# Whole-unit quanta for the last third of a dense projection that is woven into attention and a gated recurrence

## The chip, the cores and the metric

The kernel runs on one core of a Trainium2 chip (trn2). The metric is the device time of one execution in microseconds (us), as the median of three runs. The profiled execution is one of its own; its time and its span are given apart.

## The reference, cut to what matters

One inference step of a hybrid encoder layer on 2048 prompt frames and 32 new frames of a running stream (2080 rows of width 1024). After an RMSNorm one input projection feeds three head groups; their outputs are joined, projected and passed through a squared-ReLU MLP.

```
p = einsum('btd,de->bte', xn, w_in)          # 7 column groups of 512
qa, ka, va | qb, kb, vb | qc, fc, ic, gc = split(p)
oa = stick_breaking_attention(qa, ka, va)
ob = chunk_band_attention(qb, kb, vb, bias)
# HGRN2, per head a 128 x 128 state S, blocks of frames in order:
A   = (q_i * k_j * decay_ij) summed over k;  o = A v + (q exp(G)) S
S   = exp(G_last) * S + (k exp(G_last - G))^T v
oc  = rmsnorm(o) * onorm * silu(gc)
h   = x + concat(oa, ob, oc) @ w_o;  y = h + relu(rmsnorm(h) @ w_up)^2 @ w_down
```

All matrix products of the projections run as three products of a high and a low part (xhi.whi, xlo.whi, xhi.wlo), since the result has to hold float32 accuracy.

## The kernel before, in words

Three stages follow each other. `front` normalises x, keeps its transposed high and low parts and makes three of the seven column groups (QKA, VQ, KV) of the projection. `middle` is the stage of the change. `merge_and_ffn` is w_o and the MLP.

In `middle` four streams of work share all engines. **B** and **A** are the two attentions, one after the other; **C** is the recurrence (HGRN2) over 17 tiles (16 of 128 frames, one of 32), which starts when A is done. **D** (`dense`) makes the other four groups QC, FC, IC, GC that C reads, in three thirds of the rows (tiles 0 to 5, 6 to 11, and 12 to 16 with 544 columns). D's results go to memory (`scratch_tr`, `scratch_proj`) and C loads them from there tile by tile.

A D **unit** is one output block: 24 matmuls that add up in one PSUM buffer psD (8 parts of the depth times 3 products). For IC and GC a unit is 128 (or 32) rows by 256 columns, for QC and FC 128 by 272 columns in the last third. Units of one third, group and half of the columns form a **piece** (4 or 5 units in the last third), which shares one 1 MB weight load and its split into high and low parts. A unit is cut into **quanta**, stretches of matmuls that are issued together. Before, each unit of the last third has 3 quanta of 8 matmuls.

The order is written out by hand. Each stream is a generator per engine that yields after each turn. `interleave` in `middle` lays a turn of A, B or C and so many turns of D behind it into one list, `plan`, and all five engines walk through this same list. A turn of D is one quantum. What the other engines do for a unit is counted from its last quantum `z`: at turn z+1 (EVAC) ScalarE moves psD into one of three output buffers `ob` (for GC a sigmoid into `sg`); at z+2 (REFINE) VectorE works on FC or multiplies psD by the sigmoid for GC (signal `gated`); at z+3 (ONORM) GpSimd multiplies GC by a gain; at z+4 (STORE) SyncE issues the store. ScalarE waits before EVAC of unit n for the store of unit n-3. TensorE has two psD buffers, so before unit n it waits for EVAC of unit n-2, or for `gated` of unit n-2 if that is a GC unit (L645 on). SyncE loads a piece's weights at the first quantum of the piece ahead of it, first thing in the turn, after waiting for the last unit of the piece before that; the split of the weights comes at quanta 6 to 9 of that piece (`split_at`).

The last A turns belong to no new attention unit; they drain what is under way: the last transpose back (L1196), the copy L1102, the store L897. A has 196 turns and 10 quanta of the last third lie beside its last 9. C then takes a **spot** per turn, 9 spots per tile. C's first 88 spots carry the rest of D; the spots after that have none. At a spot there is a product on TensorE (L1514, 4 matmuls, one per head); one spot on, VectorE and GpSimd merge its factors into the operands of the same tile's next product (L1431, L1433, L1363), which comes two spots after, and VectorE puts the result in place (L1445, "take"). Tiles overlap, so that 8 of 9 spots have a product. Further come a transpose (L1524), the product with v (L1549, L1552), the state (L1533, L1461) and the norm and gate (L1409, L1471, L1479, L1379). SyncE loads a tile's five arrays (L1323 to L1326) 13 spots ahead.

Of the kernel before, what the change touches and what calls it, by code (L numbers as in the profile page):

```python
# [409 lines left out]
def dense(nc, sems, mp, xhi, xlo, xt, w_in, lower_bounds, onorm, psD, proj, tr):  # L410
# [31 lines left out]
    pieces, units, quanta = [], [], []  # L442
    for t, tiles in enumerate(THIRDS):
        base, n = tiles[0][0], sum(r for _, r in tiles)
        for g in ORDER[t]:
            for c in range(2):
                first = len(units)
                if g in (QC, FC):
                    for e in range(2):
                        for c0, cn in blocks_of(n):  # L450
                            units.append((t, g, 2 * c + e, base + c0, cn, len(pieces), 4 if cn > 300 else 3))
                else:
                    for t0, r in tiles:
                        units.append((t, g, c, t0, r, len(pieces), 3))
                pieces.append((t, g, c, first, len(units) - 1))
    begins, ends = [], []
    for n, u in enumerate(units):
# [6 lines left out]
    TURNS = NQ + STORE + 1  # L464
    piece_begin = [begins[p[3]] for p in pieces]

    SPLIT = 6
    split_at = {}
    for q in range(1, len(pieces)):
        for j in range(4):  # L470
            split_at[piece_begin[q - 1] + SPLIT + j] = (q, j)

    def tile_index(t, t0):
        return [z[0] for z in THIRDS[t]].index(t0)
# [22 lines left out]
    def stored_count(n):  # L497
        return 16 * sum(n_stores(k) for k in range(n % NO, n + 1, NO))
# [69 lines left out]
    def scalar(act):  # L568
        def split(q, j):
            if j == 0:  # L570
                act.wait_ge(w_loaded[q % 2], 16 * (q // 2 + 1))
                if q >= 2:
                    act.wait_ge(unit_done, pieces[q - 2][4] + 1)
            nc.scalar.activation(whi[q % 2][:, 2 * j:2 * j + 2, :], wst[q % 2][:, 2 * j:2 * j + 2, :], ACT.Copy
                                 ).then_inc(whi_ready, 1)

        for j in range(4):
            split(0, j)
        act.wait_ge(lchain, 1)
        nc.scalar.activation(lexp[:, :], lsm[:, :], ACT.Exp).then_inc(lexp_ready, 1)  # L580
        for z in range(TURNS):
            n = unit_end.get(z - EVAC)
            if n is not None:
                t, g, c, t0, r, _, _ = units[n]
                b = n % NO
                act.wait_ge(unit_done, n + 1)
                if n >= NO:

                    act.wait_ge(stored[b], stored_count(n - NO))
                ps = psD[n % NB]  # L590
                if g == QC:
                    last = nc.scalar.activation(ob[b][:, 0:r], ps[:, 0:r], ACT.Copy, scale=float(P) ** -0.5)
                elif g == FC:
                    nc.scalar.activation(ob[b][:, 0:r], ps[:, 0:r], ACT.Sigmoid)
                    last = nc.scalar.activation(sg[b][:, 0:r], ps[:, 0:r], ACT.Sigmoid, scale=-1.0)
                elif g == IC:
                    last = nc.scalar.activation(ob[b][0:r, 0:256], ps[0:r, 0:256], ACT.Copy)
                else:
                    last = nc.scalar.activation(sg[b][0:r, 0:256], ps[0:r, 0:256], ACT.Sigmoid)
                last.then_inc(act_evac, 1)  # L600
            if z in split_at:
                split(*split_at[z])
            yield

    def vector(dve):
# [20 lines left out]
        for z in range(TURNS):  # L626
            n = unit_end.get(z - REFINE)
            if n is not None:
                t, g, c, t0, r, _, _ = units[n]
# [7 lines left out]
                elif g == GC:  # L637
                    dve.wait_ge(act_evac, n + 1)
                    nc.vector.tensor_tensor(ob[b][0:r, 0:256], psD[n % NB][0:r, 0:256], sg[b][0:r, 0:256], ALU.mult
                                            ).then_inc(gated, 1)  # L640
            if z - 1 in split_at:
                split(*split_at[z - 1])
            yield

    def tensor(pe):  # L645
# [1517 lines left out]
```

## Time and profile before

| | |
|---|---|
| median of 3 runs | 3165.74 us (3161.7 to 3167.32) |
| profiled execution, its own time | 3159.14 us |
| its span on the core | 3157.4 us |
| mean granted TensorE clock | 0.977 of full |
| TensorE busy | 2965.0 us (94%) |
| VectorE busy | 1647.3 us (52%) |
| ScalarE busy | 957.8 us (30%) |
| GpSimd busy | 327.8 us (10%) |
| `middle`, A's last turns | about 1066 to 1080 us of the span |
| C with D beside it | 1087.4 to about 1275 us |
| C alone | about 1275 to 1396 us |

The busy shares say where to look at all: TensorE is busy nearly everywhere, and the stretches in which it isn't are few. They do not say what the change is worth, since the change moves matmuls from one stretch to another and removes none. That is read from the stretches themselves.

### The profile page before, as it was taken

Reading aid. Unit: us, or ns where it says so; the run is one execution under the profiler, and the core shown is the slowest. Engines: PE = TensorE matmul, PEld = TensorE weight load, DVE = VectorE, ACT = ScalarE, POOL = GpSimd, SP = SyncE. Lnnn points to the kernel's source line nnn. Section 1 sums busy time; section 2 is a strip of 40 time slices with the busy share of each in tenths; the row PEclk is TensorE's granted clock in tenths of the full one; section 3 lists DMA queues with packets and bytes.
Section 4 is the critical chain, followed back from the end, with each engine's and each line's share of the span. In section 5 each row is a group of like instructions: output and inputs, shape, how many; then the busy total and the mean of one; then the engine's idle time right before and its main releaser. Section 6 shows DMA issues by size and latency. Waiting matters only on the chain.

```text
span 3157.4 us, 45442 instructions
## 1 busy us (share of the span) xinstructions
PE 2965.0 (94%) x18200; PEld 2620.7 (83%) x18200; DVE 1647.3 (52%) x2241; ACT 957.8 (30%) x1621; POOL 327.8 (10%) x504
## 2 busy tenths in 40 slices
PE   6999799899999999859999999989999999899999
PEld 4678578788888899757889999879998998788887
DVE  4545244366566578863445444534544545455554
ACT  3322155445555322122312222222221222322221
POOL 1222110021000145630000000000000000000000
PEclk9999899999999999979999999999999999999999
DMA  6652322246222544322212112222121213222221
GB/s 207 195 188 101 101 81 75 84 131 169 79 78 72 173 144 127 116 107 87 94 54 77 57 54 94 103 71 94 57 77 54 80 67 109 96 92 83 80 81 42
DMA packets 280227, 310.23 MB, mean 98 GB/s; under 512 B 53036, under 2 KB 233870, under 8 KB 280018
## 3 DMA queue, kind: packets, MB, share of 16 engines
q1 hardware_dynamic: 280018, 307.33, 29.8%
q8 instruction: 145, 2.38, 0.3%
q14 instruction: 64, 0.52, 0.1%
HBM read 239.51 MB, written 67.78 MB: 97 GB/s over the span
## 4 chain that ended last, share of the span: by engine, by line
PE 53%; DMA 1%; DVE 1%; ACT 1%; issue 0%; SPq 0%; POOL 0%; POOLq 0%; ACTq 0%
PE mf_psO L2032 29%; PE mf_psT L2070 23%; DMA mf_nat<-scratch_mix 1%; PE mf_psT L2018 1%; DVE mf_wlo L1919 0%; ACT mf_whi L1849 0%; DVE mf_hs L1948 0%; DVE mf_acc L1942 0%; ACT mf_hs L1873 0%; ACT mf_xhi L1864 0%; DVE mf_xlo L1932 0%; DVE mf_acc L1989 0%; SPq L1794 0%; POOL mf_rstd L1840 0%; SPq L1825 0%
## 5 line engine op out<-in xcount | busy, mean ns | idle before, releaser
L1989 DVE TENSOR_TENSOR mf_acc<-mf_psO,mf_acc 128x1024 f32<-128x1024 f32 x272 | 332.9, 1224 | 382.5 <-PE mf_psO L2032 382.5
L2070 PE MATMUL mf_psT<-mf_xhi,mf_whi 128*128 128x384 f32 (+1 forms) x1536 | 492.5, 321 | 15.3 <-issue 9.9
L2070 PE MATMUL mf_psT<-mf_xlo,mf_whi 128*128 128x384 f32 (+1 forms) x1536 | 492.0, 320 | 0.0
L2070 PE MATMUL mf_psT<-mf_xhi,mf_wlo 128*128 128x384 f32 (+1 forms) x1536 | 491.9, 320 | 0.0
L2032 PE MATMUL mf_psO<-mf_whi,mf_uhi 128*128 128x512 f32 (+1 forms) x1088 | 425.8, 391 | 0.0
L2032 PE MATMUL mf_psO<-mf_whi,mf_ulo 128*128 128x512 f32 (+1 forms) x1088 | 425.3, 391 | 0.0
L2032 PE MATMUL mf_psO<-mf_wlo,mf_uhi 128*128 128x512 f32 (+1 forms) x1088 | 425.0, 391 | 0.0
L1849 ACT ACTIVATE mf_whi<-mf_st 128x2048 fp32r<-128x2048 f32 x108 | 201.8, 1909 | 639.3 <-PE mf_psO L2032 613.8
L2070 PEld LDWEIGHTS mf_psT<-mf_xhi,mf_whi 128*128 128x128 f32 x1536 | 290.4, 189 | 18.9 <-issue 16.1
L2070 PEld LDWEIGHTS mf_psT<-mf_xlo,mf_whi 128*128 128x128 f32 x1536 | 290.3, 189 | 1.8
L2070 PEld LDWEIGHTS mf_psT<-mf_xhi,mf_wlo 128*128 128x128 f32 x1536 | 290.3, 189 | 0.0
L1919 DVE TENSOR_TENSOR mf_wlo<-mf_st,mf_whi 128x2048 fp32r<-128x2048 f32 x108 | 243.5, 2289 | 63.4 <-ACT mf_whi L1849 63.4
L1977 DVE TENSOR_TENSOR mf_hs<-mf_psT,mf_hs 128x384 f32<-128x384 f32 (+1 forms) x192 | 99.2, 517 | 286.2 <-ACT mf_hs L1902 286.2
L2032 PEld LDWEIGHTS mf_psO<-mf_whi,mf_ulo 128*128 128x128 f32 (+1 forms) x1088 | 199.6, 183 | 48.6
L2032 PEld LDWEIGHTS mf_psO<-mf_wlo,mf_uhi 128*128 128x128 f32 (+1 forms) x1088 | 199.7, 184 | 46.6
L2032 PEld LDWEIGHTS mf_psO<-mf_whi,mf_uhi 128*128 128x128 f32 (+1 forms) x1088 | 199.9, 184 | 45.3
L1902 ACT ACTIVATE mf_hs<-mf_psT 128x384 f32<-128x384 f32 (+1 forms) x192 | 88.0, 459 | 403.0 <-PE mf_psT L2070 403.0
L952 ACT ACTIVATE md_wT<-md_psW 128x512 f32<-128x512 f32 (+4 forms) x232 | 128.4, 553 | 215.1 <-PE md_psW L1207 214.2
L405 PE MATMUL pj_psO<-pj_whi,xhi 128*128 128x512 f32 (+1 forms) x408 | 165.6, 406 | 13.5 <-DVE pj_wlo L327 12.1
L405 PE MATMUL pj_psO<-pj_wlo,xhi 128*128 128x512 f32 (+1 forms) x408 | 163.5, 401 | 0.0
L405 PE MATMUL pj_psO<-pj_whi,xlo 128*128 128x512 f32 (+1 forms) x408 | 163.3, 400 | 0.0
L670 PE MATMUL md_psD<-md_wlo,xhi 128*128 128x256 f32 (+1 forms) x544 | 157.6, 290 | 0.0
(185 smaller groups left out, 5305.7 us busy)
## 6 DMA issues: line engine op xcount, KB each, us to landing
mf_st<-in_w_up SPq DMA_DIRECT2D x48, 1024.0 KB, 5.8
mf_st<-in_w_down SPq DMA_DIRECT2D x48, 1024.0 KB, 4.9
md_wst<-in_w_in SPq DMA_DIRECT2D x24, 1024.0 KB, 5.4
pj_wst<-in_w_in SPq DMA_DIRECT2D x18, 1024.0 KB, 6.7
scratch_proj<-pj_ob SPq DMA_DIRECT2D x48, 256.0 KB, 2.0
mf_st<-in_w_o SPq DMA_DIRECT2D x12, 1024.0 KB, 6.1
pj_xin<-in_x_prompt SPq DMA_DIRECT2D x16, 512.0 KB, 5.6
md_qn<-scratch_proj SPq DMA_DIRECT2D x64, 128.0 KB, 2.7
```

The lines of the kernel that those rows point to most:

```text
L405: last = nc.tensor.matmul(psO[n % NO][0:r, :], xa[:, k, c], wa[m % 2][:, k, :], start=k == 0 and j == 0, stop=k == KD - 1 and j == 2)
L670: last = nc.tensor.matmul(psD[n % NB][0:r, 0:256], xa[:, k, cols], wa[q % 2][:, k, :], start=m == 0, stop=m == 23)
L952: last = nc.scalar.activation(wT[j % 4][:, 0:full, 0:r], psW[j % WB][:, 0:full, 0:r], ACT.Copy)
L1849: nc.scalar.activation(whi[wbuf(what, p)][:, :], st[m % 2][:, :], ACT.Copy).then_inc(s["whi_ready"], 1)
L1902: nc.scalar.activation(rl[k % 2][:, 0:cn], ps, ACT.Relu).then_inc(s["relu_ready"], 1)
L1919: nc.vector.tensor_tensor(wlo[b][:, :], st[m % 2][:, :], whi[b][:, :].bitcast(F32), ALU.subtract).then_inc(s["wlo_ready"], 1)
L1977: nc.vector.tensor_tensor(sq[k % 2][:, 0:cn], ps, rl[k % 2][:, 0:cn], ALU.mult).then_inc(s["sq_ready"], 1)
L1989: nc.vector.tensor_tensor(acc[0:r, i, :], psO[k % 2][0:r, :], acc[0:r, i, :], ALU.add).then_inc(s["o_out"], 1)
L2018: last = nc.tensor.transpose(psT[k % 2][:, j, 0:r], src[0:r, j * P:(j + 1) * P], ident[0:r, 0:r])
L2032: last = nc.tensor.matmul(psO[k % 2][0:r, c], xa, wa[:, c], start=j == 0, stop=j == len(steps) - 1)
L2070: last = nc.tensor.matmul(ps, wa[b4][:, w0:w0 + P], xa[:, j, c0:c0 + cn], start=j == 0 and q == 0, stop=j == KD - 1 and q == 2)
```

## The change

Each unit of the last third becomes one quantum of 24 matmuls, where it was three of 8. The thirds before keep their quanta. D has 308 quanta, where it had 380; the last third has 36, where it had 108. The split of the weights moves with the quanta: in the last third it comes one and two quanta after a piece's first, two parts at a time. Since two parts can now fall on one turn, `split_at` holds lists.

```diff
                 if g in (QC, FC):
                     for e in range(2):
                         for c0, cn in blocks_of(n):
-                            units.append((t, g, 2 * c + e, base + c0, cn, len(pieces), 4 if cn > 300 else 3))
+                            units.append((t, g, 2 * c + e, base + c0, cn, len(pieces), 1 if t == 2 else 4))
                 else:
                     for t0, r in tiles:
-                        units.append((t, g, c, t0, r, len(pieces), 3))
+                        units.append((t, g, c, t0, r, len(pieces), 1 if t == 2 else 3))
...
-    SPLIT = 6
     split_at = {}
     for q in range(1, len(pieces)):
         for j in range(4):
-            split_at[piece_begin[q - 1] + SPLIT + j] = (q, j)
+
+            at = piece_begin[q - 1] + (1 + j // 2 if pieces[q - 1][0] == 2 else 6 + j)
+            split_at.setdefault(at, []).append((q, j))
...
-            if z in split_at:
-                split(*split_at[z])
+            for q, j in split_at.get(z, []):
+                split(q, j)
...
-            if z - 1 in split_at:
-                split(*split_at[z - 1])
+            for q, j in split_at.get(z - 1, []):
+                split(q, j)
```

`middle` is untouched, and its plan counts quanta, not matmuls. Beside A's last turns there are still 10 quanta of the last third, now 10 whole units (all of IC). Beside C there were 98 quanta up to spot 83; now there are 26, up to spot 73, one every two or three spots.

The first place where this can be seen is SyncE at the end of A. Before (the rows are DMAs in the order of issue: `md_wst` is a weight load, `scratch_proj<-md_ob` the store of a unit, `scratch_mix` A's last output, `md_rcSs` and what follows C's first loads):

```order
L514 DMA md_wst_2955<-in_w_in 128x8x256 [waits dn_unit_done]
L551 DMA scratch_proj<-md_ob_2956 128x256 [waits dn_onormed,dn_unit_done]
L551 DMA scratch_proj<-md_ob_2957 128x256 [waits dn_onormed]
L551 DMA scratch_proj<-md_ob_2958 128x256 [waits dn_act_evac]
L897 DMA scratch_mix<-md_o_2986 128x256 [waits atA_o_ready]
L551 DMA scratch_proj<-md_ob_2956 128x256 [waits dn_act_evac]
L1313 DMA md_rcSs<-in_state_c 128x4x128 [waits atA_stored1,atA_stored0,atA_o_ready]
L1323 DMA md_rcq_3023<-scratch_tr 128x4x128 [waits dn_stored0,dn_stored2,dn_stored1]
```

And in the changed kernel:

```order
L515 DMA md_wst_2955<-in_w_in 128x8x256 [waits dn_unit_done]
L552 DMA scratch_proj<-md_ob_2956 128x256 [waits dn_onormed,dn_unit_done]
L552 DMA scratch_proj<-md_ob_2957 128x256 [waits dn_onormed]
L552 DMA scratch_proj<-md_ob_2958 128x256 [waits dn_act_evac]
L515 DMA md_wst_2954<-in_w_in 128x8x256 [waits dn_unit_done]
L552 DMA scratch_proj<-md_ob_2956 128x256 [waits dn_act_evac]
L552 DMA scratch_proj<-md_ob_2957 128x256 [waits dn_act_evac]
L898 DMA scratch_mix<-md_o_2986 128x256 [waits atA_o_ready]
L552 DMA scratch_proj<-md_ob_2958 128x256 [waits dn_act_evac]
L552 DMA scratch_proj<-md_ob_2956 32x256 [waits dn_act_evac]
L552 DMA scratch_proj<-md_ob_2957 128x256 [waits dn_act_evac]
L1314 DMA md_rcSs<-in_state_c 128x4x128 [waits atA_stored1,atA_stored0,atA_o_ready]
```

A second weight load has moved ahead of A's last output, and stores of units stand right behind it; three unit stores now lie between A's last output and C's first load, where one did.

The second place is VectorE beside C, at the last units of GC. Before (`md_rcqp`, `md_rctot`, `md_rcAt` are what follows a product of C; `md_ob<-md_psD,md_sg` is `gated` of a GC unit, here the one of 32 rows, and TensorE's unit two further on waits for it):

```order
L1431 TENSOR_TENSOR md_rcqp_3044<-md_rcqp_3044,md_rctot_3047 128x32x8 [waits rc_tot_ready,rc_a_ready]
L1433 TENSOR_TENSOR md_rctot_3047<-md_rctot_3047 128x32
L1445 COPY_PREDICATED md_rcAt_3060<-md_masks,md_psZ 128x512 [waits rc_taken,rc_a_ready]
L639 TENSOR_TENSOR md_ob_2958<-md_psD,md_sg_2961 32x256 [waits dn_act_evac]
L1445 COPY_PREDICATED md_rcAt_3059<-md_masks,md_psZ 128x512 [waits rc_o_done,rc_a_ready]
L1461 SCALAR_TENSOR_TENSOR md_rcS_3062<-md_rcS_3061,md_rctot_3046,md_psT 128x128 [waits rc_s_out,rc_tot_ready,rc_o_done,rc_s_done]
L1461 SCALAR_TENSOR_TENSOR md_rcS_3062<-md_rcS_3061,md_rctot_3046,md_psT 128x128 x3
L1471 TENSOR_REDUCE md_rcso_3055<-md_rcsqo_3051 128x4 [waits rc_sq_ready]
L1431 TENSOR_TENSOR md_rcqp_3044<-md_rcqp_3044,md_rctot_3047 128x16x16 [waits rc_tot_ready,rc_a_ready]
L1433 TENSOR_TENSOR md_rctot_3047<-md_rctot_3047 128x16
L1445 COPY_PREDICATED md_rcAt_3060<-md_masks,md_psW 128x512 [waits rc_taken,rc_a_ready]
L1431 TENSOR_TENSOR md_rcqp_3045<-md_rcqp_3045,md_rcf_3027 128x256 [waits rc_s_out,rc_ks_ready,rc_qp_begun,rc_a_ready]
```

TensorE begins the unit that waits for this gate behind the product whose work on VectorE starts in the last of these rows: three products after the one that the gate follows. In the changed kernel, the same gate:

```order
L1432 TENSOR_TENSOR md_rcqp_3043<-md_rcqp_3043,md_rctot_3046 128x16x16 [waits rc_tot_ready,rc_a_ready]
L1434 TENSOR_TENSOR md_rctot_3046<-md_rctot_3046 128x16
L1446 COPY_PREDICATED md_rcAt_3059<-md_masks,md_psZ 128x512 [waits rc_taken,rc_a_ready]
L640 TENSOR_TENSOR md_ob_2958<-md_psD,md_sg_2961 32x256 [waits dn_act_evac]
L1432 TENSOR_TENSOR md_rcqp_3044<-md_rcqp_3044,md_rcf_3030 128x256 [waits rc_s_out,rc_ks_ready,rc_qp_begun,rc_a_ready]
L1434 TENSOR_TENSOR md_rctot_3047<-md_rcf_3030 128x256
L1446 COPY_PREDICATED md_rcAt_3060<-md_masks,md_psZ 128x512 [waits rc_taken,rc_a_ready]
```

Here TensorE begins the waiting unit behind the product whose work starts in the fifth row: one product after the one that the gate follows. The gate and the unit that waits for it now stand on the same turn of D.

## Rows read from the trace of the kernel before

**Rows 1.** The stretches view: core, then busy us (instructions), PEclk, DMA share, GB/s
```profile
core 0: us, PE busy (x) PEld busy (x) DVE busy (x) ACT busy (x) POOL busy (x), PEclk, DMA share, GB/s
1080.00:1090.00 10.00, 2.86 (x15) 2.69 (x14) 1.17 (x2) 0.31 (x1) 2.03 (x3) 0.68 0.95 281
1087.40:1275.00 187.60, 185.93 (x1577) 184.57 (x1578) 141.14 (x272) 43.52 (x104) 93.16 (x104) 0.99 0.45 140
1296.18:1366.75 70.57, 56.18 (x460) 52.57 (x460) 61.27 (x131) 10.52 (x26) 47.09 (x56) 1.00 0.32 95
```
**Rows 2.** The stretches view for lines 667 and 670 alone, D's matmuls beside C
```profile
1087.40:1280.00 192.60, 58.55 (x384) 50.47 (x384) 0.99 0.44 137
1087.40:1280.00 192.60, 57.30 (x400) 48.99 (x400) 0.99 0.44 137
```
**Rows 3.** Timeline of GpSimd, a tile's first step: tiles 11 and 16 of C
```profile
1296.18 1.27 POOL L1352 TENSOR_TENSOR md_rcqp<-md_rcq,md_rcf 128x512 f32<-128x512 f32 x1
...
1366.75 0.45 POOL L1352 TENSOR_TENSOR md_rcqp<-md_rcq,md_rcf 128x128 f32<-128x128 f32 x1
```
**Rows 4.** Timeline of TensorE from A's last transpose into C: start, duration, [idle before]
```profile
1077.11 0.38 PE L1196 MATMUL md_psT<-md_ident,md_oT 128*128 128x128 f32 x2
1077.25 0.36 PE L670 MATMUL md_psD<-md_wlo,xhi 128*128 128x256 f32 x1
...
1080.02 0.27 PE L670 MATMUL md_psD<-md_whi,xlo 128*128 128x256 f32 x1
1087.43 2.05 PE L1514 MATMUL md_psZ<-md_rcq,md_rck 128*128 128x128 f32 x8 [7.14 <-DMA md_rcg<-scratch_proj]
1089.13 0.56 PE L670 MATMUL md_psD<-md_wlo,xhi 128*128 128x256 f32 x1
1089.49 0.41 PE L670 MATMUL md_psD<-md_whi,xhi 128*128 128x256 f32 x1
...
1090.64 0.28 PE L670 MATMUL md_psD<-md_whi,xhi 128*128 128x256 f32 x1
1090.76 0.28 PE L670 MATMUL md_psD<-md_whi,xlo 128*128 128x256 f32 x1
```
**Rows 5.** Timeline of SyncE's queue, from A's last output to C's first tile
```profile
1077.98 0.32 SPq L897 DMA_DIRECT2D scratch_mix<-md_o  x1
1079.73 0.38 SPq L1313 DMA_DIRECT2D md_rcSs<-in_state_c  x1
...
1082.60 0.43 SPq L1326 DMA_DIRECT2D md_rcg<-scratch_proj  x1
```
**Rows 6.** DMA issues of 1096.4 to 1097.2: KB each, us to landing
```profile
md_wst<-in_w_in SPq DMA_DIRECT2D x1, 1024.0 KB, 5.2
scratch_proj<-md_ob SPq DMA_DIRECT2D x1, 128.0 KB, 6.5
```
**Rows 7.** The same view of 1077 to 1079, where no weight load is ahead
```profile
scratch_proj<-md_ob SPq DMA_DIRECT2D x1, 128.0 KB, 1.8
```
**Rows 8.** Timeline of ScalarE, EVAC of one unit
```profile
1076.38 0.39 ACT L597 ACTIVATE md_ob<-md_psD 128x256 f32<-128x256 f32 x1 [3.64 <-PE md_psD L670]
```
**Rows 9.** Timeline of VectorE, a product's follow-up and a gate behind it
```profile
1257.48 0.42 DVE L1431 TENSOR_TENSOR md_rcqp<-md_rcqp,md_rctot 128x256 f32<-128x256 f32 x1
1257.82 0.83 DVE L1433 TENSOR_TENSOR md_rctot<-md_rctot 128x128 f32<-128x128 f32 x1
1258.57 0.73 DVE L1445 COPY_PREDICATED md_rcAt<-md_masks,md_psW 128x512 f32<-128x512 int32 x1
1259.18 0.42 DVE L639 TENSOR_TENSOR md_ob<-md_psD,md_sg 128x256 f32<-128x256 f32 x1
```
**Rows 10.** Timeline of TensorE: a product of C with another task right behind it
```profile
1267.63 1.05 PE L1514 MATMUL md_psZ<-md_rcq,md_rck 128*128 128x128 f32 x8
1268.52 1.06 PE L1533 MATMUL md_psT<-md_rcv,md_rckhn 128*128 128x128 f32 x8
```
**Rows 11.** DMA issues of 1050 to 1300, medians
```profile
md_rcg<-scratch_proj SPq DMA_DIRECT2D x13, 256.0 KB, 5.2
```
**Rows 12.** Waits of 1290 to 1370: us in total, times, longest
```profile
PE md_psZ L1514 <- DVE md_rcqp L1431: 7.7, 12, 0.9
PE md_psZ L1514 <- issue: 3.8, 4, 1.0
```

## The prediction

> **What bounds the kernel now.** The change touches only the last third of D, so I read the stretches view there and not the page's shares. Three stretches matter, and each has another limit [rows 1]. While D lies beside C (1087.4 to 1275 us) TensorE is busy 185.93 of 187.60 us: the sum of its matmuls bounds, and only 1.67 us are idle. Where C runs alone (five tiles, 1296.18 to 1366.75) TensorE is busy 56.18 of 70.57 us and VectorE 61.27: here the way from a product over VectorE to the next product bounds. Between A and C (1080 to 1090) TensorE is busy 2.86 of 10 us, and the granted clock shows 0.68. The change takes matmuls out of the first stretch and puts them before the third. Behind these stretches the MLP is untouched, so what C ends later the kernel ends later.
>
> **Unit prices.** D's matmuls beside C are 384 + 400 = 784, which is 98 quanta of 8 [rows 2]. From 1077.25 to 1080.02 stand 24 of them in a row; without the first step, which is longer, they follow each other at 0.117 us [rows 4]. A whole unit is 24 x 0.117 = 2.8 us. Five tiles alone take 70.57 us, which is 14.11 per tile and 1.57 per spot [rows 3]. A spot under D costs TensorE (187.6 - 784 x 0.117 - 1.67 - 1.6) / 83 = 1.12 us, where 1.6 is the slow clock at C's start (below). So a spot that loses its cover costs 0.45 us more.
>
> **The change part by part.**
>
> 1. *A's drain.* Before A's last transpose lay 7 quanta of 8 matmuls, now lie 7 units of 24: 112 matmuls more, 112 x 0.117 = **+13.1 us**. TensorE is without a gap there, so all of it counts. The drain's own steps (copies, transposes) get more cover than they need.
>
> 2. *A store behind a weight load.* The fifth and sixth DMA in the second order excerpt: SyncE waits for the end of the piece's last unit, then issues 1 MB of weights, then the store of the unit that ended three units before. ScalarE's EVAC of the unit just ended waits for that store (three output buffers), and TensorE's next unit but one waits for the EVAC (two psD). A store right behind a weight load landed after 6.5 us, one with nothing ahead after 1.8 [rows 6, 7]; the weight load itself took 5.2, which is the low end for a store queued behind it. So 0.1 + 0.4 for the issue, 5.2 to 6.5 to land, 0.4 + 0.1 for the EVAC [rows 8]: 6.2 to 7.5 us. One unit of 2.8 us covers it, and 3.4 to 4.7 remain; I take **+3.9**. Before, a unit lasted three quanta and the store had six turns of room. The ends for the range are 0 (the store overtakes the weights) and 4.7. The Trainium skill, "DMA: Bandwidth & Descriptors", section "Queues, rings and completion order", says that each DMA engine takes the descriptors of one ring in order, with no barrier on the data but with the completion signal behind all earlier writes. By that rule the store lands behind the weights and the upper end holds; rows 6 agree in one case.
>
> 3. *The gap before C.* C's first product waits for a DMA chain that hangs on A's last transpose (1077.11): copy, store L897 at 1077.98, its landing, C's loads from 1079.73, the last of the first tile issued at 1082.60, product at 1087.43 [rows 4, 5]. That is 10.3 us, of which TensorE now idles 7.14. With 72 matmuls behind the transpose (8.4 us, plus about 1 for a late EVAC) where 24 were, it idles about 1 us. C starts 10.3 us after the transpose as before: **0**. The two stores more in the queue are issued while A's output is landing. What is gained is that 48 matmuls are done inside a wait; this shows in 4.
>
> 4. *D beside C.* 98 quanta of 8 become 26 units of 24: 784 - 624 = 160 matmuls less, **-18.7 us**.
>
> 5. *The clock.* After the 7.14 us of waiting, C's first product starts the next task 1.70 us later instead of 0.89 and the next five steps of D take about 0.21 to 0.36 instead of 0.117 [rows 4, 10], together 1.6 us at the lower level (1.2 instead of 2.4 GHz). With 1 us of idling this goes: **-1.6**.
>
> 6. *Ten spots without cover.* D ends at spot 73 instead of 83: 10 x 0.45 = **+4.5**.
>
> 7. *Spots between units.* Now two or three spots follow each other without D. After a unit VectorE has caught up. The third product needs the first one's merge, which takes 0.42 on VectorE [rows 9] while the second product runs (0.89 us [rows 10]). So I cost this at nothing; the cover is the second product. At C's start nothing overlaps yet: two waits of 0.4 and 1.1 us, and 0.2 for an EVAC, **+1.7**.
>
> 8. *Gates of GC.* TensorE's unit waits for the gate that VectorE issues on the same turn, one product ahead, where it was three. A follow-up with a gate takes 2.1 us from 1257.48 on [rows 9] plus 0.15 for signals; the product that runs meanwhile takes 0.85 to 0.89. That leaves 1.4 us per unit. Of the eight units that wait for a gate, two follow a spot without a product and wait about 0.2, six wait 1.0 to 1.8: 8.8 us in all. The 1.67 us of idle time [rows 1] lie in this part and are replaced: **+7.1**. Ends: -1.7 (VectorE always ahead) and +10.
>
> 9. *ScalarE behind stores.* Each EVAC now waits for a store issued on its own turn. At weight loads and behind a tile's five loads (the last lands 5.2 us after issue [rows 11]) the store is late by 3 to 6 us. For D there is room: from a unit's end to the unit that needs its EVAC lie three spots, a unit, three spots, 9.7 us. But ScalarE's tasks for C stand behind it. By the spots, only the turn at spot 59 falls right on a tile's load and costs 1.9 us; for the others together I put 1.1: **+3.0**. Ends: 0 and +12.
>
> Sum: 13.1 + 3.9 + 0 - 18.7 - 1.6 + 4.5 + 1.7 + 7.1 + 3.0 = **+13.0 us**. The profiled execution took 3159.14 us, so the same with the change would be 3172. That execution lies 6.6 us below the median of the runs shown, a spread like theirs; the difference is what I carry over, 3165.74 + 13.0 = **3178.7 us**. What a measurement of this kernel can tell from no change is about 0.2%, 6.3 us.
>
> **Rivals.**
>
> *The cover holds.* No gate waits, no store is late: TensorE still has 2.8 us of work at each unit, and VectorE needs 61.27/45 = 1.36 us per spot, less than TensorE's 1.12 plus a third of a unit. For: VectorE has idle time in every window. Against: the order puts the gate on the waiting unit's own turn. Time: 13.1 - 18.7 - 1.6 + 4.5 - 1.7 = -4.4 us, 3161: not slower. It decides if a gate ends within 0.9 us of the product behind it.
>
> *Stores chain.* The seven tile loads beside C and five weight loads each hold ScalarE so long that C's copies come late and the chain of the recurrence stands still, 2 to 3 us each: 12 x 2.5 = 30 instead of 3, so +40 us, 3206 at most; with half of them +25, 3191. For: stores behind loads took up to 6.5 us [rows 6]. Against: 9.7 us of room. It decides if ScalarE's wait reaches past three spots and a unit.
>
> *The clock falls in the drain.* The 3.9 us of step 2 is a wait on a DMA with TensorE idle. After 7.14 us the clock was at the lower level; no row of before shows such a wait of 4 us. If it falls there too, another 1.6 us come: +14.6, 3180.3. The Trainium skill, "TensorE: Matmul & The Clock Gate", section "Loop structure matters more than you think", warns of just this, a wait for a DMA between stretches of matmuls that lets the clock drop; by it this rival holds.
>
> *C alone is not the same.* The waits there are VectorE's, 0.6 us each [rows 12]; if the ten spots fall together with gates the cost of 6 is counted twice, and the sum is +8.5, still on the slower side.
>
> **How the numbers follow.** The sum as it stands 0.40, with the fourth rival inside it; the clock rival 0.10; the cover holds 0.30; stores chain 0.20. From the first, 0.05 lies within 6.3 us, since steps 8 and 9 may both be at a third; of the cover 0.23 lies within and 0.07 beyond on the faster side, where the ends of 8 and 7 add up. So faster 0.07, same 0.28, slower 0.65. The range starts at the cover's 3161 and ends at 3196, which takes in the upper ends of 2, 8 and 9 (+27) and the smaller form of the chained stores. The forecast's own range is 3171 to 3188.
>
> **What would show it.** The gap before C at about 1 us, and the clock there near 1. A's last transpose about 17 us later than 1077.1, with a wait of about 4 us on a late EVAC some 10 us ahead of it. D's last matmul at about spot 73, ten spots earlier. Waits of TensorE at L671 for VectorE's gate, 1 to 1.8 us, six or more times. C's tiles alone unchanged at 14.11 us. Wrong would be: no wait at the gates (step 8), C's start later than 10.3 us behind the transpose (step 3), or a tile under D above 21 us before the gates start (step 9 too small).

## The result and the profile after

| | before | changed |
|---|---|---|
| median | 3164.80 us (4 runs) | 3201.95 us (4 runs, 3197.52 to 3202.64) |
| ratio to before | 1 | 1.0119 [1.0106, 1.0131] |
| span of the profiled execution | 3157.4 us | 3199.9 us |
| mean granted clock | 0.977 | 0.973 |

The change costs 37 us. I forecast 13 and a range up to 3196; the direction was right, the size not. What follows shows which terms of the sum held and which did not. The kernel before was run again beside the experiments below; its medians there lie between 3163.0 and 3166.8 us, so medians from different rounds are compared to some 4 us only.

The first look is at the stretches, in the windows view with the columns of [rows 1]. The first fence is the changed kernel, from GpSimd's first step on C's tile 0 to the same step on its tile 11 [rows 3]; the second is the kernel before between the same two steps. This stretch is called C's tiles 0 to 11 from here on.

```profile
1108.79:1334.67 225.88, 193.57 (x1544) 185.38 (x1544) 156.16 (x306) 40.96 (x104) 107.04 (x122) 0.98 0.39 120
```

```profile
1087.37:1296.18 208.81, 202.07 (x1704) 199.15 (x1704) 161.38 (x310) 47.38 (x114) 108.65 (x122) 0.99 0.44 137
```

TensorE has 160 matmuls less to do, as forecast, and yet C takes 17.1 us more. TensorE was idle for 6.7 us there, now for 32.3. Its busy time fell by only 8.5 us, where 160 matmuls at 0.117 us are 18.7: the matmuls that are left take longer too.

The end of A, TensorE's timeline of the changed kernel, which answers to [rows 4]:

```profile
1093.93 0.58 PE L671 MATMUL md_psD<-md_whi,xhi 128*128 128x256 f32 x1 [3.52 <-ACT md_ob L598]
...
1098.35 0.38 PE L1197 MATMUL md_psT<-md_ident,md_oT 128*128 128x128 f32 x2
...
1101.92 0.39 PE L671 MATMUL md_psD<-md_whi,xhi 128*128 128x256 f32 x1 [0.39 <-ACT md_ob L598]
...
1108.85 1.13 PE L1515 MATMUL md_psZ<-md_rcq,md_rck 128*128 128x128 f32 x8 [1.02 <-DMA md_rcg<-scratch_proj]
```

SyncE issued one weight load at 1068.82, where the last third begins, and a second at 1087.64, with two unit stores right behind it:

```profile
1087.64 0.38 SPq L515 DMA_DIRECT2D md_wst<-in_w_in  x1
1088.07 1.05 SPq L552 DMA_DIRECT2D scratch_proj<-md_ob  x2
```

And ScalarE's timeline shows who stood between: the EVAC waited 9.43 us for a store.

```profile
1093.51 0.72 ACT L598 ACTIVATE md_ob<-md_psD 32x256 f32<-32x256 f32 x2 [9.43 <-DMA scratch_proj<-md_ob]
```

TensorE then resumed at the lower clock, granted 0.50 (windows view):

```profile
1093.90:1097.20 3.30, 3.27 (x15) 3.27 (x16) 0.00 (x0) 1.36 (x3) 0.00 (x0) 0.50 0.00 0
```

From the first weight load (the start of the last third) to A's last transpose: before 1077.11 - 1065.87 = 11.2 us, now 1098.35 - 1068.82 = 29.5. From the transpose to C's first tile: 10.3 before, 1108.79 - 1098.35 = 10.4 now.

What waits beside C, the waits view of the changed kernel over 1108.79 to 1334.67 (TensorE):

```profile
PE md_psD L671 <- DVE md_ob L640: 12.4, 7, 3.4
PE md_psZ L1515 <- DVE md_rcqp L1432: 7.3, 10, 1.6
PE md_psT L1534 <- ACT md_rckhn L1404: 4.0, 3, 2.7
...
PE md_psD L668 <- ACT md_ob L598: 1.4, 1, 1.4
```

and of ScalarE, of 1060 to 1330, where before not one wait for a store was shown:

```profile
ACT md_ob L598 <- DMA scratch_proj<-md_ob: 26.4, 3, 10.7
...
ACT md_ob L595 <- DMA scratch_tr<-md_sg: 21.8, 3, 9.6
ACT md_sg L600 <- DMA scratch_proj<-md_ob: 21.4, 2, 10.8
...
ACT md_ob L593 <- DMA scratch_tr<-md_ob: 14.6, 2, 9.5
```

With three smaller groups these are 102.8 us of waiting in 13 waits. Two of the 13, 9.43 and 6.22 us, lie before C's start; 87.1 us lie beside C. One of them, in full. SyncE issues a tile's five loads from 1155.57 on, C's output, 1 MB of weights at 1158.59 and only then three unit stores, all in one queue. The stores land 7.9 us after their issue, against 1.8 with nothing ahead [rows 7] (DMA issues of 1155.5 to 1159.0, then of 1159 to 1161.5):

```profile
md_wst<-in_w_in SPq DMA_DIRECT2D x1, 1024.0 KB, 8.5
...
scratch_mix<-md_rcon SPq DMA_DIRECT2D x1, 256.0 KB, 6.1
```

```profile
scratch_tr<-md_ob SPq DMA_DIRECT2D x3, 136.0 KB, 7.9
```

ScalarE waits 9.53 us and does C's copy (L1404) only behind it:

```profile
1167.59 0.40 ACT L593 ACTIVATE md_ob<-md_psD 128x272 f32<-128x272 f32 x1 [9.53 <-DMA scratch_tr<-md_ob]
1167.88 0.59 ACT L1404 ACTIVATE md_rckhn<-md_psW 128x512 f32<-128x512 f32 x1
```

and TensorE's state product waits for that copy, then runs 1.75 us where it ran 1.06 [rows 10], since the clock has fallen meanwhile:

```profile
1168.53 1.75 PE L1534 MATMUL md_psT<-md_rcv,md_rckhn 128*128 128x128 f32 x8 [2.67 <-ACT md_rckhn L1404]
```

The clock fell three times in this stretch (windows view). Ahead of the second and third fall TensorE had waited 2.02 and 3.45 us for gates, and ran some matmuls at 1.00 first (1249.68 to 1250.70, 1283.43 to 1284.90).

```profile
1168.50:1171.70 3.20, 3.17 (x17) 3.18 (x17) 1.39 (x5) 2.06 (x5) 0.00 (x0) 0.57 0.02 5
1250.50:1254.00 3.50, 3.50 (x20) 2.88 (x19) 0.00 (x0) 0.00 (x0) 0.00 (x0) 0.55 1.01 303
1284.50:1288.00 3.50, 3.50 (x21) 3.50 (x20) 0.00 (x0) 0.00 (x0) 0.00 (x0) 0.57 0.00 0
```

These are 10.2 us at a mean of 0.56, which cost about 4.5 us against 1.00 (an estimate from these rows). Another wait of 2.02 us, at 1275.58, was followed by no fall.

C alone is what it was: from the start of tile 11 to that of tile 16 it takes 1405.25 - 1334.67 = 70.58 us, against 70.57 [rows 3].

### The profile page after: what moved, and what is told of

The parts are those of the page before. It is cut to its first block, busy times and chain, and to the rows that moved or that the text cites. A ratio compares the mean times of both kernels' runs of the same rounds, so it can differ in the third digit from the quotient of the medians.

```text
span 3199.9 us, 45442 instructions
## 1 busy us (share of the span) xinstructions
PE 2986.7 (93%) x18200; PEld 2635.0 (82%) x18200; DVE 1644.3 (51%) x2241; ACT 955.8 (30%) x1621; POOL 326.0 (10%) x504
## 4 chain that ended last, share of the span: by engine, by line
PE 52%; DMA 1%; DVE 1%; ACT 1%; issue 0%; SPq 0%; POOL 0%; POOLq 0%; ACTq 0%
PE mf_psO L2033 28%; PE mf_psT L2071 23%; DMA mf_nat<-scratch_mix 1%; PE mf_psT L2019 1%; DVE mf_wlo L1920 0%; ACT mf_whi L1850 0%; DVE mf_hs L1949 0%; DVE mf_acc L1943 0%; ACT mf_hs L1874 0%; ACT mf_xhi L1865 0%; DVE mf_xlo L1933 0%; DVE mf_acc L1990 0%; SPq L1795 0%; POOL mf_rstd L1841 0%; SPq L1826 0%
## 5 line engine op out<-in xcount | busy, mean ns | idle before, releaser
L405 PE MATMUL pj_psO<-pj_whi,xhi 128*128 128x512 f32 (+1 forms) x408 | 166.2, 407 | 12.3 <-DVE pj_wlo L327 12.0
L671 PE MATMUL md_psD<-md_whi,xhi 128*128 128x256 f32 (+1 forms) x544 | 159.2, 293 | 16.3 <-DVE md_ob L640 12.4
```

What stands on the lines that cost most here:

```text
L405: last = nc.tensor.matmul(psO[n % NO][0:r, :], xa[:, k, c], wa[m % 2][:, k, :], start=k == 0 and j == 0, stop=k == KD - 1 and j == 2)
L671: last = nc.tensor.matmul(psD[n % NB][0:r, 0:256], xa[:, k, cols], wa[q % 2][:, k, :], start=m == 0, stop=m == 23)
```

## The experiments

Three theories stood against each other, and the clock turned out to belong to each of them. **Stores**: ScalarE's EVAC waits for a store issued on its own turn, and C's copies queue behind it. **Gates**: TensorE's unit waits for VectorE's gate of the same turn. **Cover**: spots without D wait for VectorE, either those at the end of D or the runs between whole units.

### More buffers, or earlier stores

The first kernel has four output buffers instead of three.

```diff
-    NO = 3
+    NO = 4
```

> The changed kernel with four output buffers of D instead of three, so that ScalarE's EVAC of unit n waits for the store of unit n-4, issued one turn of D earlier. Store theory (the 37 us come mostly from EVACs that wait for a store issued on their own turn, 117 us of such waits on ScalarE, which hold the copies of the recurrence behind them): 15 to 25 us below the changed kernel, 3177 to 3187, and ScalarE's waits for stores fall below 20 us. Gate theory (TensorE's waits for VectorE's gate on the same turn, 12.4 us, carry it): at most 3 us below. Cover theory (spots without D beside them are the loss): no change, 3202.

Measured 3184.82 us, ratio to before 1.0075 [1.0059, 1.0091]: 17 us of the 37 are gone. ScalarE's waits for stores over 1060 to 1330 fell from 102.8 us (not the 117 of the expectation) to 31.5, not below 20. C's tiles 0 to 11 took 212.77 us, 13.1 less; the 3.52 us wait before the transpose is gone as well.

```profile
1101.94:1314.71 212.77, 188.83 (x1544) 181.68 (x1544) 155.70 (x306) 42.07 (x103) 107.36 (x121) 0.99 0.42 127
```

Of the 13.1 us, 8.4 are idle time of TensorE and 4.7 busy time of the same 1544 matmuls. The idle part is mainly 5.4 us of waits for ScalarE (C's copies and an EVAC), now none, and 2.7 of gate waits: 9.7 in 6 cases, the longest 2.0 where it was 3.45. Ahead of that gate ScalarE had waited 10.56 us for a store. The clock falls once there, for about 4 us at 0.59, not three times; that is about 3 of the 4.7 us (an estimate from these rows).

The second keeps three buffers and issues the stores earlier.

```diff
+    stores_at = {}
+    for n, u in enumerate(units):
+        lag = {QC: 2, IC: 2, FC: 3, GC: 4}[u[1]] if u[0] == 2 else STORE
+        stores_at.setdefault(ends[n] + lag, []).append(n)
...
-            n = unit_end.get(z - STORE)
-            if n is not None:
+            for n in stores_at.get(z, []):
```

> The changed kernel with each store of the last third issued as early as its data allow: QC and IC two turns behind the unit, FC three, GC four as before. Store theory: for QC, IC and FC the waits go, for GC they stay: 12 to 20 us below the changed kernel, and the 3.5 us wait of TensorE before A's last transpose goes. Gate theory: the GC stretch is untouched and keeps its cost, 0 to 4 us below. Cover theory: no change.

Measured 3188.10 us, ratio 1.0081 [1.0062, 1.0100], 14 us gained; C's tiles 0 to 11 took 217.84 us. TensorE has no wait for an EVAC left before the transpose; its gate waits are still 9.7 us. Two different ways around the same wait give nearly the same time: the store theory holds for somewhat under half of the loss.

### The gate out of the output buffer

```diff
+                    nc.scalar.activation(ob[b][0:r, 0:256], ps[0:r, 0:256], ACT.Copy)
                     last = nc.scalar.activation(sg[b][0:r, 0:256], ps[0:r, 0:256], ACT.Sigmoid)
...
-                    nc.vector.tensor_tensor(ob[b][0:r, 0:256], psD[n % NB][0:r, 0:256], sg[b][0:r, 0:256], ALU.mult
+                    nc.vector.tensor_tensor(ob[b][0:r, 0:256], ob[b][0:r, 0:256], sg[b][0:r, 0:256], ALU.mult
...
-                        if units[n - NB][1] == GC:
-                            pe.wait_ge(gated, upto(n - NB, GC))
-                        else:
-                            pe.wait_ge(act_evac, n - NB + 1)
+                        pe.wait_ge(act_evac, n - NB + 1)
```

> The changed kernel, where ScalarE copies a GC unit to its output buffer as well as taking the sigmoid, and VectorE multiplies there; TensorE then waits for ScalarE's EVAC alone and never for the gate. Same results, one more ScalarE operation of 0.4 us per GC unit. Gate theory: the 12.4 us of waits for the gate go, 10 to 12 us below the changed kernel, 3190 to 3192. Store theory: TensorE's gate waits are partly the store waits handed on (the gate waits for the EVAC), so they come back as waits for the EVAC: 0 to 5 us below.

Measured 3199.61 us, ratio 1.0115 [1.0097, 1.0133]: within the intervals the changed kernel. (The profiled execution was the fastest of its four, 3192.91 us; its C took 220.04 us for tiles 0 to 11, 5.8 less.) The gate waits are gone, but in their place stands a wait for the EVAC, itself held by a store (waits of TensorE, 1109.82 to 1329.86):

```profile
PE md_psD L669 <- ACT md_sg L601: 5.2, 1, 5.2
```

There the stores hold ScalarE, and the gate is not the last to end. With four buffers as well:

> The changed kernel with both: four output buffers and the gate of GC out of the output buffer (TensorE waits only for ScalarE's EVAC). The four-buffer kernel alone took 3184.8 us and still had 9.7 us of TensorE's waits for the gate. Gate theory for the rest: those 9.7 us go, 3174 to 3178. If the gate waits only took the place of other waits of the recurrence's own chain (spots without D between whole units): at most 4 us below 3184.8.

Measured 3173.78 us, ratio 1.0025 [1.0016, 1.0035], 11 us below four buffers alone by the medians, about 16 by the ratios. The gate theory is right for this part. C's tiles 0 to 11 take 204.36 us (8.4 less).

The third step adds early stores to that.

> The changed kernel with four output buffers, early stores and the gate out of the output buffer, so that neither stores nor gates hold a whole unit. What remains over before is the price of whole units and of their place alone: my prediction's terms without stores and gates, 13.1 - 18.7 - 1.6 + 4.5 + 1.7 = -1.0 us, 3162 if they are right. If runs of spots without D cost more than I put (step 7 at nothing), 3170 or more.

Measured 3175.46 us, ratio 1.0035 [1.0022, 1.0049]. Nothing more comes, though ScalarE's waits for stores beside C fell from 26.4 to 12.3 us. It is 3175, not the 3162 of my terms, so whole units have a price of their own. A part of it is the clock: in this profile TensorE waited 2.91 us for C's first load and ran the next 5.7 us at a granted 0.50, and it fell again behind D's last matmul.

### The place of the units

Of the ten units beside A's last nine turns three stay, the other seven go to C's share.

```diff
+        last = [i for i, kind in enumerate(plan) if kind == "A"][-9]
+        kept = 0
+        for i in range(last, len(plan)):
+            if plan[i] == "D":
+                kept += 1
+                plan[i] = "D" if kept % 3 == 1 and kept < 9 else ""
+        plan[last:] = [kind for kind in plan[last:] if kind]
-        interleave("C", TAIL, Dn.turns - upto_a)
+        interleave("C", TAIL, Dn.turns - plan.count("D"))
```

> The changed kernel with 3 whole units beside A's last nine turns instead of 10, and 33 beside C instead of 26, which is about the number of matmuls that each place had before. Cover theory: D again covers the spots as far as before, most of the loss goes, 3168 to 3178. Store theory: each further unit beside C brings its own wait, the time stays within 6 us of the changed kernel's 3202 or above it. The gap before C is back at about 5 to 7 us.

Measured 3206.09 us, ratio 1.0137 [1.0119, 1.0155]. More D beside C did not help. In the profile ScalarE waited 108.1 us for stores in 14 waits, the longest 17.5; but that execution was the slowest of the four (3219.27 us), with a granted clock of 0.92 in C, so its waits may be larger than the typical ones. The cover theory in the form "too few matmuls beside C" promised 3168 to 3178 and falls; how much more cover was worth by itself this run can't tell, since the store waits came with it.

The opposite test keeps quanta of 8 and moves the same ten units to A's end:

```diff
+        last = [i for i, kind in enumerate(plan) if kind == "A"][-9]
+        tail = plan[last:]
+        plan[last:] = [k for kind in tail for k in ([kind] * 3 if kind == "D" else [kind])]
-        interleave("C", TAIL, Dn.turns - upto_a)
+        interleave("C", TAIL, Dn.turns - upto_a - 2 * tail.count("D"))
```

> The kernel before, with its quanta of 8 matmuls, but 30 of them beside A's last nine turns instead of 10, which puts the same 10 units (240 matmuls) there as in the changed kernel; 78 quanta remain beside C, spread to spot 83. It keeps the place and undoes the grain. If the place is to blame: 3175 or more. If the grain is (whole units as one turn of all engines' order): 3163 + 13.1 - 18.7 - 1.6 = 3156, faster than before, since the gap before C is filled and D still covers 83 spots.

Measured 3164.44 us, ratio 1.0001 [0.9991, 1.0010]. The place costs nothing. It brings nothing either: C's tiles 0 to 11 took 192.95 us, where 208.81 less the moved matmuls and the slow start would be 188.5. The slow start did not go: C's first load was issued 4.1 us behind the transpose, TensorE waited 2.90 us for it, and the first 2 us of C ran at a granted 0.50.

### What the grain costs by itself

The uncoupled kernel (four buffers, gate out of the buffer, 3173.78 us) with D spread wider:

```diff
-        LEAD, TAIL = 6, 88
+        LEAD, TAIL = 6, 95
```

> The kernel with four output buffers and the gate out of the output buffer (3173.8 us), with its units spread over C's first 95 spots instead of 88, so that D ends at spot 80 instead of 73. Late-spots theory (the rest of the loss is the ten spots that lost their cover at D's end, 0.45 us each): 3 us less, 3170 to 3171. Runs theory (what costs is that two or three spots follow each other without D wherever they are, each run waiting for VectorE): no change, 3173 to 3175.

Measured 3171.58 us, ratio 1.0020 [1.0010, 1.0029]; the intervals overlap, but C's tiles 0 to 11 went from 204.36 to 200.42 us, near the 3 us of the late spots. Then the uncoupled kernel with two quanta of 12 per unit, and TAIL at 88 again:

```diff
-                            units.append((t, g, 2 * c + e, base + c0, cn, len(pieces), 1 if t == 2 else 4))
+                            units.append((t, g, 2 * c + e, base + c0, cn, len(pieces), 2 if t == 2 else 4))
...
-                        units.append((t, g, c, t0, r, len(pieces), 1 if t == 2 else 3))
+                        units.append((t, g, c, t0, r, len(pieces), 2 if t == 2 else 3))
...
-            at = piece_begin[q - 1] + (1 + j // 2 if pieces[q - 1][0] == 2 else 6 + j)
+            at = piece_begin[q - 1] + (3 + j if pieces[q - 1][0] == 2 else 6 + j)
...
+        last = [i for i, kind in enumerate(plan) if kind == "A"][-9]
+        tail = plan[last:]
+        plan[last:] = [k for kind in tail for k in ([kind] * 2 if kind == "D" else [kind])]
-        interleave("C", TAIL, Dn.turns - upto_a)
+        interleave("C", TAIL, Dn.turns - upto_a - tail.count("D"))
```

> The same kernel with quanta of 12 matmuls, two per unit, four output buffers, the gate out of the output buffer, and the same 10 units (now 20 quanta) beside A's last nine turns; beside C a quantum on two of three spots. Runs theory: the runs of spots without D shrink to one, 6 to 10 us less, 3164 to 3168. Late-spots theory: D ends at spot 80, 3 us less at most, 3170 to 3174.

Measured 3166.97 us, ratio 1.0000 [0.9991, 1.0010]: the whole loss is gone with the matmuls at the same place. C's stretch, first of the whole-unit kernel, then of the half-unit one:

```profile
1103.71:1308.07 204.36, 188.86 (x1544) 183.04 (x1544) 156.91 (x306) 44.62 (x113) 108.47 (x121) 0.98 0.44 132
```

```profile
1102.47:1296.23 193.76, 183.38 (x1544) 179.95 (x1544) 159.05 (x306) 45.59 (x113) 112.26 (x121) 1.00 0.45 138
```

The same 1544 matmuls, 10.6 us apart. Three or four are the late spots (D ends at spot 80, not 73; the wider spread gave 3.9). The rest lies in two places. Divided at D's last matmul, the whole-unit kernel shows:

```profile
1103.71:1268.50 164.79, 158.00 (x1318) 154.54 (x1319) 124.13 (x239) 38.38 (x97) 81.50 (x90) 1.00 0.46 140
1268.50:1308.07 39.57, 30.86 (x229) 28.50 (x227) 32.78 (x67) 6.24 (x16) 26.98 (x31) 0.91 0.35 101
```

Behind D's end the clock fell, which the half-unit kernel is spared (below). While D is there, TensorE idles 6.8 us. I estimate that about 5 of the 10.6 us belong to that part, the runs of spots without D between units: the half-unit kernel's D ends at 1269.8, 167.3 us into C, with 7 spots of 1.12 us more in it. One thing more differs. Halving the units also halves every lag counted in turns, and ScalarE's waits for stores beside C went from 26.4 us to none. That these count for little is seen from the kernel with early stores as well: half of them went there, and C took 206.75 us, of which about 2.8 are the slow clock at its start.

In the whole-unit kernel TensorE waits for VectorE's merge 14 times, in the half-unit one 11 times (waits of TensorE, whole units first):

```profile
PE md_psZ L1513 <- DVE md_rcqp L1430: 8.0, 11, 1.8
PE md_psZ L1513 <- issue: 2.7, 5, 1.0
PE md_psW L1513 <- DVE md_rcqp L1430: 2.4, 3, 1.1
PE md_psW L1513 <- issue: 1.4, 5, 0.4
```

```profile
PE md_psZ L1513 <- DVE md_rcqp L1430: 6.2, 7, 1.2
...
PE md_psW L1513 <- DVE md_rcqp L1430: 2.2, 4, 0.9
PE md_psZ L1513 <- issue: 1.0, 1, 1.0
PE md_psW L1513 <- issue: 0.4, 1, 0.4
```

The shown waits differ by 4.7 us, of which only 2.0 are waits for the merge, and TensorE's busy time by 5.5, for the same matmuls. About 3.0 of the 5.5 are the clock (an estimate from the row below): it fell once in the whole-unit kernel, behind D's end, after waits of 0.37, 0.65 and 1.83 us between products, and is 1.00 over C in the half-unit kernel.

```profile
1274.30:1280.70 6.40, 5.03 (x22) 4.69 (x23) 4.22 (x10) 0.60 (x1) 4.72 (x7) 0.53 0.91 268
```

What the other 2.5 us are is not shown; a product that ends in a stop counts 1.13 to 1.16 us of busy time, where the next task begins after 0.89 if one is ready.

### The wait alone

The last run of this line asks whether late stores do harm without whole units, gates or another place.

```diff
-    TURNS = NQ + STORE + 1
+    TURNS = NQ + 10 + 1
...
+        stores_at.setdefault(ends[n] + (10 if u[0] == 2 else STORE), []).append(n)
...
-        LEAD, TAIL = 6, 88
+        LEAD, TAIL = 6, 93
```

> The kernel before, with quanta of 8 matmuls and every matmul at its place, but each store of the last third issued ten turns of D behind the unit instead of four, which is the turn on which ScalarE's EVAC of the unit three further on waits for it, as in the changed kernel. Gates, place and grain stay as before. Store theory (the wait alone holds C, whatever the grain): ScalarE waits for stores 80 us and more beside C, TensorE waits for ScalarE's copies, 12 to 18 us over before, 3176 to 3184. If the store waits hurt only together with whole units: within 4 us of before, though ScalarE waits as long.

Measured 3196.40 us, ratio 1.0099 [1.0082, 1.0116]. The wait by itself, with matmuls, quanta and gates as before, costs 30 us, twice what I expected. The stretch of C's tiles 0 to 11, then ScalarE's largest waits beside C:

```profile
1089.44:1326.97 237.53, 212.19 (x1704) 206.88 (x1704) 155.48 (x310) 45.52 (x114) 106.32 (x121) 0.96 0.40 121
```

```profile
ACT md_ob L595 <- DMA scratch_tr<-md_ob: 24.8, 3, 9.2
ACT md_ob L597 <- DMA scratch_tr<-md_sg: 23.1, 3, 10.0
ACT md_ob L600 <- DMA scratch_proj<-md_ob: 20.6, 2, 11.8
```

Together with four smaller groups they are 103.2 us, all beside C, where the changed kernel has 87.1. C takes 28.7 us more than before: 18.6 are idle time of TensorE, and 10.1 are busy time for the same 1704 matmuls, at a clock of 0.96 instead of 0.99. In four stretches of together 19.2 us the granted clock is 0.52 to 0.59; the first follows a wait of 4.50 us for an EVAC. So a late store is paid twice, in waiting and in the clock behind it.

Why the waits cost more here than the 13 to 17 us that taking them away gained in the changed kernel is open beyond that. Gates and late copies may overlap in the changed kernel, so that removing one leaves the other. The medians point that way (2 us for the gate with the stores in place, 11 without), the profiled stretches of C only weakly (5.8 and 8.4), and neither proves it.

### The gap before C, without the change

The gap of 7.14 us before C [rows 4] is the one thing that the change does fill. First with quanta of 8 alone:

```diff
+        plan.extend(["D"] * 8)
-        interleave("C", TAIL, Dn.turns - upto_a)
+        interleave("C", TAIL, Dn.turns - upto_a - 8)
```

> The kernel before with 8 quanta of 8 matmuls placed between A's last turn and C's first spot, taken from C's share. They fill the 7.14 us for which TensorE waits for C's loads: 64 x 0.117 = 7.5 us of work moves into the wait and the slow clock behind it (1.6 us) goes, 3163 - 7 - 1.6 = 3154 to 3156. If the loads come later by as much, or the spots lose cover: 3163.

Measured 3169.93 us, ratio 1.0015 [1.0005, 1.0025]: no gain, and if anything a little slower. The gap only moved, since SyncE too took the eight turns of D ahead of C's first load:

```profile
1096.89 2.05 PE L1514 MATMUL md_psZ<-md_rcq,md_rck 128*128 128x128 f32 x8 [7.87 <-DMA md_rcg<-scratch_proj]
```

```profile
1087.36 0.38 SPq L1313 DMA_DIRECT2D md_rcSs<-in_state_c  x1
```

The load comes 9.0 us behind the transpose (1078.36), where it came 2.6 behind it [rows 4, 5]. Then SyncE alone takes C's first turn ahead of those quanta:

```diff
+        first_c = plan.index("C")
+        load_first = plan[:first_c - 8] + ["C"] + ["D"] * 8 + plan[first_c + 1:]
...
-            run(Dn.sync(sp), B.sync(sp), A.sync(sp), C.sync(sp))
+            run(Dn.sync(sp), B.sync(sp), A.sync(sp), C.sync(sp), plan=load_first)
```

> The kernel before with 8 quanta between A and C as in the run that filled the gap (3169.9 us, where C's loads stood in SyncE's order behind the unit stores of those quanta and began 7.6 us later), but SyncE alone takes C's first turn, with its loads, ahead of those quanta. If SyncE's order was what gave the gain back: C starts 10 to 11 us behind A's last transpose again, 7.5 us of work lie in the wait, 3155 to 3159. If the spots of C lose as much for want of D: 3162 to 3165.

Measured 3162.26 us, ratio 0.9985 [0.9976, 0.9994]: an interval below 1, by 0.15% and not by the 0.3% that the gap holds; that is less than the 0.2% named in the prediction, so a gain that is small at best. C's first load is again 2.6 us behind the transpose (1081.43 and 1078.81), TensorE no longer waits for it, and tiles 0 to 11 take 204.9 us instead of 208.8, where 9.1 us less were due. So about half of what the gap gave was lost again in C. That it was for want of D is argued only: TensorE's waits for the merge rose from 5.1 to 7.7 us there, but ScalarE also waited 10.7 us for two stores, of which the kernel before has none.

## Why the prediction was wrong

The whole difference of the two profiled spans is 42.5 us. The stages ahead account for 2.9 (the first weight load of the stretch) and the MLP, which is untouched, for 4.0 (3199.9 - 1405.25 against 3157.4 - 1366.75); such differences between executions come in unchanged stages (over the fourteen profiles the MLP's stretch took 1790.7 to 1798.1 us, with the kernel before at the low end). The stretch of the change holds 35.6: 18.3 in the drain, 0.2 to C's first tile, 17.1 in C under D, 0 in C alone.

- **Steps 1 and 2, the drain: held.** Forecast 17.0, measured 18.3. The wait behind the weight load was 3.52 us, for 3.9 forecast; the store landed 5.2 us after issue. The wait came 4.4 us ahead of the transpose, not 10. With four buffers the wait went and the drain took 24.3 us, 13.0 more than before, which is step 1 alone. What the sum left to a rival is the clock: after that wait the 22 steps from one matmul to the next between 1094.31 and 1098.23 took 3.92 us, where 0.117 us each makes 2.6. The clock did fall to the lower level, and it cost 1.3 us. The Trainium skill, "TensorE: Matmul & The Clock Gate", section "Loop structure matters more than you think", warns that a long wait for a DMA between matmuls lets the clock drop. The trace agrees: 3.52 us of waiting, here for an EVAC that a store held, stand ahead of the slow matmuls.
- **Step 3, the gap: held.** C starts 10.4 us behind the transpose, TensorE idles 1.02 and 0.39 us.
- **Step 4, 160 matmuls less: held** (1704 and 1544 in the stretches).
- **Step 5, the clock: held at C's start** (the granted clock is 1.00 from 1108.85 to 1111.00), but the sum asked after the clock nowhere else in C, and it fell there three times, for about 4.5 us. In the accounts below this is inside the terms whose waits stand ahead of it.
- **Step 8, the gates: right in mechanism and nearly in size.** 12.4 us of waits in 7 cases for 8.8 forecast; taken away with the stores out of the way they gained 8.4 us in C and 11 in all, for 7.1 net. The longest, 3.45 us, was partly a store's.
- **Step 9, ScalarE behind stores: this is where the sum failed first.** Forecast +3.0, measured 13.1 in C by the four-buffer run and up to 15.7 with the gate gone too (220.04 to 204.36, the former from a quick execution). I compared the delay with the room that D has, 9.7 us, and walked through C's tasks for one spot only. The waits were up to 10.8 us, not 3 to 6, and in the case followed above a tile's loads, C's output and a weight load stood in the queue together. And what ScalarE owes to C has no such room: TensorE waited 2.67, 0.56 and 0.74 us for its copies. About 3 of the 13.1 us are the clock that fell behind such waits. The sign that I had named for this came: tile 3 took 25.2 us under D, before the gates start, where it took 20.3. The rival "Stores chain" had this mechanism; it put the stores at 30 us, or at half of that, and the half is what the runs gave back. The Trainium skill, "DMA: Bandwidth & Descriptors", section "Queues, rings and completion order", says that each DMA engine takes the descriptors of one ring in order. This speaks for that rival, and the 7.9 us of the stores behind the loads agree.
- **Steps 6 and 7, spots without cover: step 7, "I cost this at nothing", failed.** Together I put 6.2 us and took 1.6 off for the clock. With stores and gates out of the way C took 204.36 us, against 208.81 - 18.7 + 4.6 = 194.7: 9.7 us more. Of these the half-unit run gives all back, while the wider spread gives 3.9. VectorE's mean load leaves room, but between units TensorE waits up to 1.1 us for a merge, and behind D's end up to 1.8; about 3 us of the 9.7 are the clock that fell behind D's end. The division of the rest is an estimate.

The misses add up to what was measured: 1.3 in the drain, 0.2 before C, 10.1 in step 9, 1.3 in step 8 and 9.7 in steps 6 and 7 are 22.6 us on top of 13.0, which gives the 35.6 of the stretch. The range was also added up wrongly: the upper ends of steps 2, 8 and 9 give 13.0 + 0.8 + 2.9 + 9.0 = 25.7 us, not 27, and it held nothing for the clock beside C or for the runs of step 7.

Steps 8 and 9 were treated as a sum. By the medians they are not one: the gate alone gained 2 us, the gate after the stores 11. By the stretches of C in the profiles it was 5.8 and 8.4, so the size of the overlap is open.

## What to carry to other kernels

In an order shared by all engines, the length of a turn is also the distance between a result and its use. Making turns three times as long leaves every lag in turns unchanged but shifts the engines against each other: a wait that had two turns of room in between can land on the turn of its own releaser. Before changing a quantum, list for each wait how many turns lie between it and its releaser on the other engine's list; those at zero are the first suspects. Here one more buffer gave back 17 of the 37 us, an earlier store 14.

When an engine serves two streams in one order, a delay must be compared with the room of the other stream, not only of the one that waits. And a wait of TensorE is to be priced with the clock behind it.

## What was not expected of the hardware

Stores of 136 KB queued behind 1.25 MB of tile loads, 256 KB of C's output and 1 MB of weights landed 7.9 us after issue, and the 1 MB load itself then took 8.5 us where it took 5.2 to 5.6 before. Short waits cost more than their length: after 3.52 us of waiting for an EVAC TensorE ran 3.3 us at a granted 0.50. Beside C the clock fell after waits of 2.67, 2.02 and 3.45 us, the last two times only 1.0 and 1.5 us after the matmuls had resumed, while another wait of 2.02 us was followed by none.
